# Queries, key scores and picks of the first token half in one block, in two groups of heads

## The reference, cut to what matters

```python
def peer(h, w_query, sub_keys, expert_u, expert_v):
    ...
        q = (xb @ w_query).reshape(T, PEER_HEADS, 2, PEER_HALF)
        s = jnp.einsum('thpk,hpnk->thpn', q, sub_keys).astype(jnp.float32)
        top_s, top_i = lax.top_k(s, PEER_TOPK)
        cand_s = top_s[:, :, 0, :, None] + top_s[:, :, 1, None, :]
        ...
        best_s, best_pos = lax.top_k(cand_s.reshape(T, PEER_HEADS, PEER_TOPK * PEER_TOPK), PEER_TOPK)
        ...
        gate = jax.nn.softmax(best_s, axis=-1)
        u = expert_u[idx]
        v = expert_v[idx]
        act = jax.nn.gelu(jnp.einsum('td,thkd->thk', xb, u).astype(jnp.float32), approximate=False)
        return jnp.einsum('thk,thkd->td', (gate * act).astype(xb.dtype), v)
```

## Time and profile before

| | us |
|---|---|
| median of 3 executions | 3736.01 |
| lowest, highest | 3730.77, 3745.04 |
| span of the profiled execution, first to last instruction | 3649.2 |
| median less that span: what lies around it | 86.8 |
| VectorE busy in the span | 2141.9 |
| TensorE busy in the span | 2696.2 |
| GpSimd busy in the span | 1315.4 |

### The profile page before, as it was taken

The page is one execution under the profiler, slowest core; times in us unless marked ns, Lnnn a source line. Parts: engine busy times, 40 slices in busy tenths (PEclk is TensorE's granted clock), DMA queues, the critical chain, the costliest instruction groups (busy, mean ns, idle before and its releaser), DMA issues. The chain is left out here.

```text
span 3649.2 us, 44644 instructions
## 1 busy us (share of the span) xinstructions
PE 2696.2 (74%) x17746; PEld 1944.6 (53%) x17746; DVE 2141.9 (59%) x3992; ACT 587.5 (16%) x1213; POOL 1315.4 (36%) x1082
## 2 busy tenths in 40 slices
PE   5977433657992066799975657799999789777787
PEld 4867323555430055688863546578888567322232
DVE  5543898878776987999987988333222443100001
ACT  1031001210000012222222200132222321100001
POOL 0000258567776766677764656200000000000000
PEclk7989667778996578799987778989999889889998
DMA  7613579689999989799998799523332325899997
GB/s 272 237 35 116 192 265 390 216 322 380 357 366 376 379 310 351 274 397 399 395 341 276 251 364 353 185 69 108 99 100 85 116 93 195 334 428 428 428 428 321
DMA packets 390750, 1006.31 MB, mean 276 GB/s; under 512 B 30381, under 2 KB 234515, under 8 KB 375699
## 3 DMA queue, kind: packets, MB, share of 16 engines
q0 software_dynamic: 150912, 549.52, 40.3%
q1 hardware_dynamic: 211856, 406.65, 30.3%
q10 hardware_dynamic: 27779, 47.38, 3.6%
HBM read 971.99 MB, written 31.46 MB: 275 GB/s over the span
## 5 line engine op out<-in xcount | busy, mean ns | idle before, releaser
L1427 POOL DMA_INDIRECT ring<-in_peer_u_dram,index x512 | 683.7, 1335 | 435.8 <-DVE ring L1505 198.4
L1427 POOL DMA_INDIRECT ring<-in_peer_v_dram,index x512 | 602.5, 1177 | 294.4 <-DVE h_rows_b L1511 135.9
L345 PE MATMUL bank<-hT,weights 128*128 128x256 f32 x2240 | 505.2, 389 | 175.7 <-DMA weights<-in_w_in_dram 84.3
L345 PEld LDWEIGHTS bank<-hT,weights 128*128 128x128 f32 x2240 | 436.9, 196 | 243.3 <-issue 103.8
L1821 PE MATMUL bank<-hT,weights 128*128 128x256 f32 x1792 | 420.8, 389 | 4.0 <-DVE weights L2019 4.0
L1821 PEld LDWEIGHTS bank<-hT,weights 128*128 128x128 f32 x1792 | 336.4, 192 | 54.2 <-DVE weights L2019 4.4
L1505 DVE SCALAR_TENSOR_TENSOR ring<-ring,h_rows_a 128x1024 f32<-128x1024 f32 x256 | 304.7, 1221 | 64.4 <-DMA ring<-in_peer_u_dram,index 62.4
L1511 DVE SCALAR_TENSOR_TENSOR h_rows_b<-ring,coef,h_rows_b 128x1024 f32<-128x1024 f32 x238 | 305.1, 1282 | 46.9 <-DMA ring<-in_peer_v_dram,index 27.9
L1505 DVE SCALAR_TENSOR_TENSOR ring<-ring,h_rows_b 128x1024 f32<-128x1024 f32 x256 | 299.8, 1224 | 5.0 <-DMA ring<-in_peer_u_dram,index 4.5
L2838 POOL IOTA mo_down<- 128x4 f32 x1 | 0.1, 144 | 789.6 <-POOLq L160 789.6
L1524 PE MATMUL bank<-ring,weights 128*128 128x512 f32 x512 | 223.3, 597 | 9.3 <-DVE weights L1499 9.0
(11 more groups left out here) (562 smaller groups left out, 4097.8 us busy)
## 6 DMA issues: line engine op xcount, KB each, us to landing
weights<-in_w_in_dram SPq DMA_DIRECT2D x112, 512.0 KB, 3.9
weights<-in_w_in_dram SPq DMA_DIRECT2D x54, 1024.0 KB, 9.7
xp_near<-in_w_exp_gate_dram SPq DMA_DIRECT2D x9, 4096.0 KB, 33.7
xp_far<-in_w_exp_up_dram SPq DMA_DIRECT2D x9, 4096.0 KB, 33.0
xp_near<-in_w_exp_up_dram SPq DMA_DIRECT2D x7, 4096.0 KB, 33.9
xp_far<-in_w_exp_gate_dram SPq DMA_DIRECT2D x7, 4096.0 KB, 35.7
xp_near<-in_w_exp_down_dram SPq DMA_DIRECT2D x7, 4096.0 KB, 34.5
xp_far<-in_w_exp_down_dram SPq DMA_DIRECT2D x7, 4096.0 KB, 32.8
```

The lines of the kernel that those rows point to most:

```text
L345: ins = pe.matmul(m.ps[b][:, 0:TH], m.weights[:, s, k, c * P:(c + 1) * P], rhs(k), start=(k == 0), stop=(k == k_tiles - 1))
L1427: pool.indirect_dma_start(out=self.ring[:, n % RING, :], out_offset=None, in_=self.tables[table], in_offset=bass.IndirectOffsetOnAxis(ap=s ...
```

## The change

The first half gets a block of its own, `queries_and_picks`, in place of the projection and `key_scores`; `key_scores` stays for the second half.

- TensorE makes query tiles 0 to 7, scores heads 0 to 3 of tile 0 into banks 4 and 5, makes tiles 8 to 15 (in banks 0 to 3, as the first eight), scores heads 4 to 7 of tile 0 into banks 6 and 7, then all of tile 1 into banks 0 to 3.
- ScalarE copies the query tiles, after the stores of zeros; then comes the exponential of heads 0 to 3, then the copies of tile 1's scores into `half.h`.
- VectorE loads the scores of tile 0 straight from the banks, picks heads 0 to 3 in full, and heads 4 to 7 up to part 2 (`SOON = 3`). Parts 3 to 13 of heads 4 to 7 and the load of tile 1 from `first.h` (`load_tiles`) become the setup of the next projection, in the stretch.
- SyncE loads the first four chunks of `w_in` into the slots, as the query tiles free them.
- GpSimd issues its first twelve gathers in this block.

```diff
-def first_mixer(m, half, columns, w_in, w_out, masks, carry, work, then, hook=None, other=None, hook2=None, other2=None, other3=None):
+def first_mixer(m, half, columns, w_in, w_out, masks, carry, work, then, setup=None, hook=None, other=None, hook2=None, other2=None, other3=None):
...
-                hook=hook, other=other)
+                setup=setup, hook=hook, other=other)
...
+def queries_and_picks(m, half, w_query, kT, qT, picker, peer, zeros, then):
...
+        @block.sync
+        def _(sp):
+            for s in range(SLOTS):
+                sp.wait_ge(m.tile_made, made0 + (s + 1) * per_slot)
+                sp.dma_start(m.weights[:, s, :, :],
+                             wv[:, :, (SLOTS + s) * SLOT_COLS:(SLOTS + s + 1) * SLOT_COLS]).then_inc(m.w_landed[s], 16)
+            prefetch(m, sp, *then, done=lambda s: made0 + per_turn + (s + 1) * per_slot)
+            zeros.wait(sp)
+
+        @block.gpsimd
+        def _(pool):
+            peer.gather(pool, 0, RING)
...
+            for q in range(PT):
+                s, c, turn = q // per_slot % SLOTS, q % per_slot, q // per_turn
+                pe.wait_ge(m.w_landed[s], landed0[s] + 16 * (turn + 1))
+                if q >= 4:
+                    pe.wait_ge(m.tile_kept, kept0 + q - 3)
+                for k in range(KT):
+                    ins = pe.matmul(m.ps[q % 4][:, 0:TH], m.weights[:, s, k, c * P:(c + 1) * P], half.h[:, k, :],
+                                    start=(k == 0), stop=(k == KT - 1))
+                ins.then_inc(m.tile_made, 1)
+                if q % PH == PH - 1:
+                    for hp in range(q - PH + 1, q + 1):
+                        pe.wait_ge(m.tile_kept, kept0 + hp + 1)
+                        ins = score(0, hp, m.ps[4 + hp // 4])
+                        if hp % 4 == 3:
+                            ins.then_inc(scored, 1)
+            for hp in range(PT):
+                ins = score(1, hp, m.ps[hp // 4])
+                if hp % 4 == 3:
+                    ins.then_inc(scored, 1)
+
+        @block.scalar
+        def _(act):
+            zeros.store(act)
+            for q in range(PT):
+                act.wait_ge(m.tile_made, made0 + q + 1)
+                act.copy(qT[:, q, :], m.ps[q % 4][:, 0:TH]).then_inc(m.tile_kept, 1)
+            picker.exp(act, 0, early_heads)
+            for b in range(4):
+                act.wait_ge(scored, 4 + b + 1)
+                act.copy(half.h[:, 2 * b:2 * b + 2, :], m.ps[b][:, :].rearrange("p (k t) -> p k t", t=TH)).then_inc(copied, 1)
+            act.wait_ge(copied, 4)
+
+        @block.vector
+        def _(dve):
+            m.pool.wait(dve)
+            for b in range(2):
+                dve.wait_ge(scored, b + 1)
+                picker.load(dve, b * 4, m.ps[4 + b][:, :])
+            for n in range(picker.PARTS):
+                picker.part(dve, n, 0, early_heads)
+            for b in range(2, 4):
+                dve.wait_ge(scored, b + 1)
+                picker.load(dve, b * 4, m.ps[4 + b][:, :])
+            for n in range(picker.SOON):
+                picker.part(dve, n, 0, late_heads)
...
     PARTS = 14
+    SOON = 3
...
+    def load_tiles(self, dve, scores):
+
+        self.m.dve.link(dve, dve.tensor_copy(self.s[:, :, :].rearrange("p (k j) n -> p k (j n)", k=KT), scores))
...
+        if half.first:
+            queries_and_picks(m, half, w_query[0], keys.T, qT, picker, peer, zeros, then)
+            return
...
+                    def pick_rest(dve):
+                        late_heads = picker.turns(0)[1]
+                        for n in range(picker.SOON, picker.PARTS):
+                            picker.part(dve, n, 0, late_heads)
+                        picker.load_tiles(dve, first.h)
+
                     def exp_next(block, made0, kept0):
                         @block.scalar
                         def _(act):
+                            picker.exp(act, 0, picker.turns(0)[1])
                             picker.exp(act, 1)
...
-                                    hook=pick_next, other=exp_next)
+                                    setup=pick_rest, hook=pick_next, other=exp_next)
```

More of the change, by code:

```diff
@@ L1132, in _, with score @@
                 m.act.mark(act.copy(self.T[:, 4 * b:4 * b + 4, :].rearrange("p j n -> p (j n)"), m.ps[4 + b][:, :]))
-def key_scores(m, half, kT, qT, s_all, picker, peer, zeros):
-    nc = m.nc
-    HP = 2 * PH
+def queries_and_picks(m, half, w_query, kT, qT, picker, peer, zeros, then):
+    PT = 2 * PH
+    wv = w_query.rearrange("(k p) n -> p k n", p=P)
+    per_slot, per_turn = SLOT_COLS // P, SLOTS * (SLOT_COLS // P)
+    assert m.ahead == SLOTS and PT == 2 * per_turn
+    m.ahead = 0
+    made0, kept0, landed0 = m.tile_made_n, m.tile_kept_n, list(m.w_landed_n)
+    scored, copied = m.sem("keys_made"), m.sem("scores_copied")
+    early_heads, late_heads = picker.turns(0)
+    with in_block(m) as block:
+        @block.sync
[9 more added lines that the diff above has]
+            peer.gather(pool, 0, RING)
+        @block.tensor
+        def _(pe):
+            def score(t, hp, bank):
+                return pe.matmul(bank[:, (hp % 4) * P:(hp % 4 + 1) * P], qT[:, hp, t * P:(t + 1) * P], kT[:, hp, :],
+                                 start=True, stop=True)
+            for q in range(PT):
[41 more added lines that the diff above has]
+                picker.part(dve, n, 0, late_heads)
+    m.tile_made_n += PT
+    m.tile_kept_n += PT
+    for s in range(SLOTS):
+        m.w_landed_n[s] += 32
@@ L1140, in key_scores @@
+def key_scores(m, half, kT, qT, s_all, picker):
     i0 = HT * half.j
     made, first_kept, s_kept = (m.sem(f"keys_{x}") for x in ("made", "first_kept", "s_kept"))
[L1142 to L1165, removed]
-                for b in range(4):
[L1167 to L1200, removed]
@@ L1611, in along, with store, first_experts @@
         return clear
[L1613 to L1618, removed]
+    def store(self, act):
+        act.wait_ge(self.cleared, 1)
+        for b in range(self.blocks):
+            act.dma_start(self.dst[b * P:(b + 1) * P, :], self.src).then_inc(self.stored, 16)
     def wait(self, sp):
         sp.wait_ge(self.stored, 16 * self.blocks)
-def first_experts(m, half, w_query, sub_keys, picker, rows, peer, y_rest=None):
+def first_experts(m, half, w_query, sub_keys, picker, rows, peer, y_rest=None, then=None):
     zeros = None if y_rest is None else Zeros(m, peer.rows[1][:, 0, :], y_rest)
@@ L3600, in two_blocks @@
                                 other3=sum_rest)
-                    first_experts(m, first, peer_w_query, peer_sub_keys, picker, rows[0], peer, y_rows[PAIRS * P:, :])
+                    first_experts(m, first, peer_w_query, peer_sub_keys, picker, rows[0], peer, y_rows[PAIRS * P:, :],
+                                  (w_in[0], 12, 16 * P))
                 with nc.Block() as block:
```

46 lines of the change are left out of this document (41 added, 5 removed).

## The result

The changed kernel takes 3705.45 us, the kernel before 3738.87 on the same chip (medians of four executions each, 3694.85 to 3719.79 and 3730.77 to 3745.04): a ratio of 0.9907 with a 95% interval of 0.9881 to 0.9932. The prediction said 3702.8 and faster. The number held; one step of its working did not, and the time alone would not have told.

A forecast was written before the change was run, and what follows sets the result against it. TensorE's queries and VectorE's picks ran in sequence, then VectorE's fixed order bound the kernel. Gains 31.1 and 12.2, less 1.2, 1.5, 5.9 and a 1.5 boundary, gave 33.2 us: span 3616.0 plus 86.8, 3702.8 us; range 3687 to 3720.

The forecast's parts named there:

- The early start: In the query block, the first part of the early picks begins at 324.1 and not 355.16, 31.1 us earlier.
- The exponential: In the early picks, VectorE waits for ScalarE's exponential of heads 0 to 3 and loses 1.2 us.
- the bank loads: In the block, VectorE's two loads of scores from banks for heads 4 to 7 cost 1.5 us.
- the three terms: Losses up to the block end: 1.2 us for the exponential, 1.5 for bank loads, 5.9 for GpSimd.
- The end of the block: The other engines wait 5.9 us for GpSimd to issue twelve gathers, by 366.9; VectorE goes on at 368.4.
- another case: In the block, the twelve gathers take 1.68 us each, ending at 375.8: 3712 us; chance 0.10 together with the landings.
- that rival: At the block end, GpSimd waits for its gathers to land, 6.1 us more: about 3709; chance 0.10 together with slower gathers.
- GpSimd's pace: In the block, the twelve gathers take 14.9 us as before, mostly 0.94 us each, once 1.09.
- The rest of the late picks: Behind the block, parts 3 to 13 take 22.2 us and tile 1's load 1.22; first copy at 391.9.
- Downstream: Behind the first copy, the whole shift of 33.2 us stays to the end of the span.
- Little clock was lost late: Rival from 2500 to 3050: a lower TensorE clock takes the gain, 3736 or 3771; little or none 0.08, slower 0.04.
- The 86.8 us around the span: Time outside the traced span, taken as untouched by the change and added to 3616.0 to give 3702.8.

The follow-up runs named there:

- e6_exp_early: Changed kernel with ScalarE's exponential of heads 0 to 3 one query tile earlier: 3627.29 us, ratio 0.9924 to the kernel before.
- e0_before: The kernel before, unchanged, traced again: 3657.05 us, ratio 1.0007.
- e1_after: The changed kernel, unchanged, traced again on another chip: 3623.88 us, ratio 0.9913 to the kernel before.
- e4_soon6: Changed kernel with SOON = 6 in place of 3, so parts 3 to 5 of heads 4 to 7 are in the block: 3626.38 us, ratio 0.9917.
- e8_no_prefetch: Changed kernel with the four w_in loads left to the start of the next projection: 3716.4 us, ratio 0.9926 to the kernel before.
- e9_soon8: Changed kernel with SOON = 8 in place of 3, so parts 3 to 7 of heads 4 to 7 are in the block: 3708.39 us, ratio 0.9901.
- e2_gathers_out: Changed kernel with the first twelve gathers moved out of the block, behind its end: 3609.86 us, ratio 0.9879 to the kernel before.
- e10_soon8_again: The kernel of e9_soon8 (SOON = 8), unchanged, run again on another chip: 3607.95 us, ratio 0.9882 to the kernel before.
- e5_soon13: Changed kernel with SOON = 13 in place of 3, all parts of heads 4 to 7 but the last in the block: 3615.8 us in one execution.

## Why the prediction was right, and where it was wrong

**The early start** was right within 1 us. Parts begin at 323.25 (324.1 forecast), the first gather goes out at 351.19 (352.0). TensorE never stood between its fourth and fifth tile. ScalarE's copies took 0.37 us and not 0.42.

**The exponential** was right in size, 1.05 us against 1.2, and wrong as a term that shifts anything. Behind it stood a longer wait that doesn't depend on it, so it cost nothing (e6_exp_early). The same holds for the 1.5 us of the bank loads: by the prediction's own working GpSimd ended at 366.9 whatever VectorE did, and only the sum of the three terms, 8.6 us, was one of the path. The table load took its 1.28 us and the exponential started 0.01 us behind it, so the 1.38 us of drain that the Trainium skill (ScalarE: Activation LUTs, "What ACT_TABLE_LOAD costs") puts on top isn't seen here.

**The end of the block** is the step that failed. The prediction took "issues only, since an engine otherwise goes on behind a transfer that it has issued", had VectorE go on at 368.4 and charged 5.9 us. The block waits for the landing, 5.5 us behind the last issue (365.95 to 371.42); 0.8 of this came back from the earlier start and 0.3 from issues and boundary. VectorE went on at 372.8, 4.4 us later, which is the whole difference between the 33.2 forecast and the 28.8 measured at the first copy. That the medians moved by 33.4 all the same is luck: their interval reaches from 25 to 44 us, and on the next chip they moved by 28.4. The landing stood in the prediction as a bound, 6.1 us on top and 3709 in time, with a chance of 0.10 shared with another case. By mechanism that rival happened. The error lies in the choice between the two: "an engine goes on" is true between gathers and says nothing of the end of a block, where it isn't enough that GpSimd has issued all that it has. The earlier trace rows show no case of GpSimd last, but the trace that they come from did hold the answer, in the closing instruction that ended at 404.1: 6.1 us behind the last issue and 0.54 behind the last landing. With the landing in the sum neither verdict nor sign would have changed, since 3702.8 and 3709 both lie within the interval measured.

**GpSimd's pace** was right: gathers of 0.94 us with 0.30 between, once 1.09, beside copies from banks and picks. The two added copies didn't slow it. They read a bank, at 0.69 us for 512 columns, where the copy inside of SBUF takes 1.22 us for 2048. The Trainium skill (SBUF — State Buffer, "Who interferes with whom") says that a VectorE instruction with at most one input in SBUF, outside of its two-port modes, doesn't contend with GpSimd, and the 0.94 us beside these copies agree. Beside dot products they took 1.68 us again (the thirteenth, at 401.17).

**The rest of the late picks** was right to 0.1 us: 22.2 and 1.22 forecast, 372.79 to 396.23 measured. The load from the token half takes its 1.22 us in eight pieces as in one. TensorE was not waited for.

**Downstream** was right: the shift stays whole within a few us (e0_before and e1_after). Little clock was lost late: from 2575 to 2875 us the granted clock is 1.00 and from 2875 to 3125 it is 0.89, where the earlier trace rows have 1.00 and 0.90:

```profile
2575.00:2875.00 300.00, 300.00 (x3807) 257.73 (x3803) 82.16 (x143) 79.54 (x147) 0.00 (x0) 1.00 0.34 99
2875.00:3125.00 250.00, 213.28 (x1269) 167.29 (x1268) 105.04 (x203) 67.07 (x158) 0.00 (x0) 0.89 0.40 136
```

**The 86.8 us around the span** was wrong: only 1.8 us lie there in each execution that was timed and traced. The rest is, by all that these runs show, the difference between a trace from one chip and a median from another. It did no harm only because it went into both sides of a subtraction. A gap of that size between a span and a time should have been named as unexplained.

## What to carry to other kernels

The block that held gathers of GpSimd closed when the last had landed, not when it was issued. Where another kernel's trace shows the same, put work of the other engines beside the landing, or the gathers behind the boundary, and look which engine closes a block before paying for anything ahead of it. A wait is worth its length only where nothing longer ends behind it; measure from an event just ahead of the edit to one just behind it, since 1 us could be told so here, and in the total 5 us could not (e4_soon6). Where a span and a median differ by two per cent, look whether they are from the same chip before reasoning on either.

## What the runs showed of the hardware that was not expected

**Chips differ.** The kernel before takes 3652.3, 3659.7 and 3651.8 us on three chips and 3738.9 and 3741.7 in the two other comparisons. Most of it arises in the mixer of the second network block: the changed kernel's first trace is 29 us behind e1_after's at 1559 us, 85 at 1954.5, and 72 at the end. Two windows of that part, between the same matmuls, first on the slower chip, then on the faster (columns as in the earlier trace rows), and TensorE's waits at the line with the largest difference in each (us in total, times, longest):

```profile
1664.00:1954.00 290.00, 263.83 (x2992) 221.46 (x2986) 235.64 (x349) 67.38 (x135) 185.87 (x144) 0.92 0.88 326
```

```profile
PE bank L2194 <- issue: 19.2, 36, 1.1
```

```profile
1612.00:1869.00 257.00, 242.79 (x2998) 207.73 (x2998) 236.09 (x351) 66.40 (x134) 191.56 (x145) 0.97 1.00 375
```

```profile
PE bank L2194 <- issue: 0.9, 1, 0.9
```

The same work takes 290 us and 257. On the slower chip TensorE stands 36 times with nothing shown that it waits for, and the granted clock is 0.92, not 0.97. VectorE has idle times of the same kind: over 14 us in sum in each of the three traces from the slower chips (the changed kernel's first, e8_no_prefetch and e9_soon8), and at most 2.1 in each of the eleven from the others. In the block of the picks they fall where the gathers land. What an engine waits for there was not settled, and that it goes with the chip is an association of three traces against eleven.

**The bare boundary** between the two blocks costs 1.4 us from VectorE's last instruction to its next (e2_gathers_out with no gather in flight, e9_soon8 and e10_soon8_again with all landed), and 1.64 once (e5_soon13). VectorE's last instruction in e10_soon8_again ended at 371.80, GpSimd's closing one at 371.79.
